# Four modulation units in one run of products behind one weight unit, where they stood as two pairs

## Chip, core and metric

One Trainium2 chip, one of its cores. The metric is the device time of one execution, in microseconds (us). The kernel works on float32 data throughout.

## What is computed

Two transformer blocks, one after the other, on 256 positions of width 2048. The first has a mixer (a gated linear recurrence and sparse attention), a feed-forward part and a gated extra input. The second has two layers that work on two streams, x and a context, and each scales, shifts and gates both by numbers that it makes from two vectors, `c` and `c_ctx`: the modulation. Cut to what the change touches:

```python
# first block, feed-forward part
f = jnp.square(jax.nn.relu(rms_norm(h, norm_mlp_pre[i]) @ mlp_w1[i])) @ mlp_w2[i]
h = h + rms_norm(f, norm_mlp_post[i])
...
# second block, for each of its two layers l
shift, scale, gate = jnp.split((s_lat @ w_mod[l] + b_mod[l])[:, None, :], 3, axis=-1)
shift_c, scale_c, gate_c = jnp.split(s_ctx @ w_mod[l] + b_mod[l], 3, axis=-1)
hx = _rmsnorm(x, norm_g[l]) * (1.0 + scale) + shift
hc = _rmsnorm(ctx, norm_g[l]) * (1.0 + scale_c) + shift_c
```

`w_mod` is 2048 x 6144 for each layer. Nothing of it depends on the feed-forward part, so the kernel makes most of it beside that part.

## The kernel before

All weights stream from HBM through a ring of four slots, `raw`, in **units** of 1 MB (128 partitions x 4 tiles of rows x 512 columns). `HAND` is the list of all units in the order in which SyncE (SP) fetches them; SP issues unit n only when unit n - 4, which had the same slot, is done with.

There are two kinds of unit. A **weight unit** is split in two halves of its own: ScalarE (ACT) makes the rounded high part `whi` (line 1415, two instructions, one for each half), VectorE (DVE) makes the rest, `wlo` (line 2001), and the slot is free when the second low half is made (`lo_ready`). `whi` and `wlo` have two places each, so a half is split only when TensorE (PE) has used the same half of the weight unit two before (`unit_used`). PE then runs 24 products of 128x512 (`hand_unit`, lines 724 to 726). A **modulation unit** is not split: PE multiplies the raw float32 tiles by two columns of `cvec` (`mod_products`, line 772, four products that lie side by side in the array), and the slot is free when they are done (`plain_used`). The profile has two records for each of these products, so a unit is 8 records there and a pair is 16.

The feed-forward part has 128 weight units, n = 0 to 127 (even groups of 16 from the up projection `mlp_w1`, odd ones from the down projection `mlp_w2`). From n = 4 on they are counted in groups of seven, m_ = (n - 4) // 7 and at = (n - 4) % 7. Each group m_ = 0 to 15 makes one chunk of 512 columns of `w_mod` out of four modulation units. For m_ = 0 to 11 PE does it, into PSUM bank 3; the last four (`SUMS`) are summed on DVE. Behind the fourth unit:

- for m_ = 0 to 3 (`ROWS`) ACT copies two rows out and DVE adds them (`mod_row`);
- for m_ = 4 to 11 (`COLS`) ACT copies the bank to `modp_b` (line 1433) and PE turns it by four transposes (line 779). The transposes stand behind the weight unit with at = 5. The copy stands in ACT's program behind the split of the weight unit with at = 6.

```python
                if at == 6 and m_ in COLS:
                    mod_part(MODSS + m_, MOD1[4 * m_ + 3], modp_b, 3)
```

ACT's loop over the weight units n does first `hand_split(x)`, then `beside(n - 2)` (small work for the attention of the context: exponentials at line 1697, squares at line 1710), then the line above. PE too has such small work behind some weight units (lines 1029 to 1132).

Of the kernel before, what the change touches and what calls it, by code (L numbers as in the profile page):

```python
# [41 lines left out]
MODSS = 2 * D // CH  # L42
# [6 lines left out]
MODB = [(0, MODSS + i) for i in range(MODCH - MODSS)] + [(1, i) for i in range(MODCH)]  # L49
# [13 lines left out]
STEP_AT = [13 + 3 * n // 2 for n in range(len(STEP))] + [37, 38, 39]  # L63
N_VEC, N_CONST = 1 + 18 + 2, 3 + 4
MOD1_AT = 4
SUM_AT = (1, 2, 4, 5)
MOD0_AT = [(3 + 4 * m, 4 + 4 * m, 5 + 4 * m, 5 + 4 * m) for m in range(8)]

# [29 lines left out]
def build(nc, I, out):  # L98
    ctx = ExitStack()
    with ctx:  # L100
# [347 lines left out]
        order = []  # L448
# [2 lines left out]
        order += ["in2_0c"] * 5 + ["cmp", "in2_0c", "in2_0c"] * 4 + ["in2_0c"] * 35  # L451
        order += ["out1"] * 16 + ["in2_0c"] * 4
        for n in range(128):
            order += ["mlp"] + (["mod1"] * 2 if MOD1_AT <= n < 7 * len(MODB) + MOD1_AT and (n - MOD1_AT) % 7 in (1, 4) else [])
        order += ["out2_0c"] * 8 + ["gate", "gate", "pp", "gate", "gate"] * 4 + ["out2_0c"] * 8
        for l in range(2):
            order += (["in2_1c"] * 16 if l else []) + [f"in2_{l}x"] * 52 + [f"out2_{l}"] * 16
# [16 lines left out]
        SUMS = [m_ for m_, (l, col) in enumerate(MODB) if l and col >= MODSS]  # L474

        def before(those, m_):
            return len([i for i in those if i < m_])
# [100 lines left out]
        def ev(name):  # L578

            if name not in one_shot:  # L580
                one_shot[name] = sem(name)
            return one_shot[name]
# [106 lines left out]
        def _(pe):  # L689
# [17 lines left out]
            def hand_unit(x, A, middle=None):  # L707

                hi_, lo_ = A
                by_rows = x.u in (0, UPC - 1) and x.s > 0  # L710
                for i in range(2 * TB):
                    b, kh = (i // 2, i % 2) if by_rows else (i % 2, i // 2)
                    a, bank = half(x, b)
                    if b == 0:
                        pe.wait_ge(lo_ready, 2 * x.s + kh + 1)
                    if x.u == 0 and a >= 3 and kh == 0:
                        pe.wait_ge(half_out, a - 2)
                    if i == 2 and middle is not None:
                        middle()
                    tt = slice(b * P, b * P + P)  # L720
                    dst = ps[:, bank, :]
                    for k in range(2 * kh, 2 * kh + 2):
                        kk, nth = UK * x.k + k, UK * x.u + k
                        mm(dst, hi_[:, kk, tt], whi[:, x.s % 2, k, :], start=(nth == 0), stop=False)  # L724
                        mm(dst, hi_[:, kk, tt], wlo[:, x.s % 2, k, :], start=False, stop=False)  # L725
                        ins = mm(dst, lo_[:, kk, tt], whi[:, x.s % 2, k, :], start=False, stop=(nth == KT - 1))  # L726
                    if x.u == UPC - 1 and (b, kh) == (0, 1):
                        ins.then_inc(half_done, 1)
                    if b == 1:
                        ins.then_inc(unit_used, 1)  # L730
# [37 lines left out]
            def mod_products(y, bank):  # L768

                pe.wait_ge(raw_in[y.slot], y.landed)  # L770
                for k in range(UK):
                    ins = mm(ps[32 * k:32 * k + 32, bank, :], cvec[:, UK * y.u + k, :], raw[:, y.slot, k],  # L772
                             start=(y.u == 0), stop=(y.u == UPC - 1))
                ins.then_inc(plain_used, 1)

            def mod_columns(modp, bank):

                for j in range(4):
                    ins = nc.tensor.transpose(ps[:, bank, j * P:j * P + P], modp[:, j * P:j * P + P], eye[:, :])
                ins.then_inc(ev("modc_sum"), 1)  # L780
# [240 lines left out]
            def turn(x, c):  # L1021

                zp = (x.i // 8 * 4 + c) % 2
                pe.wait_ge(relu_sq, 2 * (x.i // 8 * 4 + c + 1))
                if x.i or c:
                    pe.wait_ge(hT_lo, x.i // 8 * 4 + c)
                for k in range(UK):
                    for b in range(TB):
                        ins = nc.tensor.transpose(ps[:, 4 + k // 2, ((k % 2) * TB + b) * P:((k % 2) * TB + b + 1) * P],  # L1029
                                                  zst[:, zp, b, k * P:k * P + P], eye[:, :])  # L1030
                ins.then_inc(hT_psum, 1)
# [113 lines left out]
            for n, x in enumerate(MLP):  # L1145
                q, j = x.i // 8, x.i % 8
                if x.u == 2 and 1 <= j <= 4:
                    turn(x, j - 1)
                if x.i == 0:
                    pe.wait_ge(a_lo, PR["mlp"]["t0"] + 2 * (x.u + 1))  # L1150
                if j == 4:
                    pe.wait_ge(hT_lo, q * 4 + x.u + 1)
                hand_unit(x, AX_ if j < 4 else AY_)
                m_, at = (n - MOD1_AT) // 7, (n - MOD1_AT) % 7
                if at == 5 and m_ in SUMS:
                    pe.wait_ge(plain_used, MOD1[4 * m_ + 3].p + 1)
                    pe.wait_ge(ev("modc_set"), MODSS + len(COLS))
                    pe.wait_ge(ev("mod_row"), len(ROWS) - len(SUMS))
                    pe.wait_ge(ev("mod_part"), before(ROWS, m_))
                    mm(ps[0:32, 3, :], ones[:, 0:32], modp_b, start=True, stop=True).then_inc(ev("modc_sum"), 1)  # L1160
                if 0 <= m_ < SUMS[0] and at in (1, 4):
                    if at == 1 and m_:
                        pe.wait_ge(ev("modc_set"), MODSS + before(COLS, m_))
                        pe.wait_ge(ev("mod_row"), before(ROWS, m_))
                    for u in ((0, 1) if at == 1 else (2, 3)):
                        mod_products(MOD1[4 * m_ + u], 3)
                elif m_ in COLS and at == 5:
                    pe.wait_ge(ev("modp_in"), MODSS + before(COLS, m_) + 1)
                    mod_columns(modp_b, 3)
                beside(n)  # L1170
                if n == 120:
                    pe.wait_ge(ev("p_in"), 16)
                    for k in range(2):
                        for b in range(TB):
                            ins = nc.tensor.transpose(ps[:, 3, (k * TB + b) * P:(k * TB + b + 1) * P],
                                                      prow[:, b, k * P:k * P + P], eye[:, :])
                    ins.then_inc(ev("pT_made"), 1)
# [192 lines left out]
        def _(act):  # L1370
# [270 lines left out]
            def hT_part(c):  # L1641

                act.wait_ge(hT_psum, c + 1)
                act.wait_ge(unit_used, 2 * MLP[32 * (c // 4)].s)
                A(ay_hi[:, UK * (c % 4):UK * (c % 4) + UK, :].rearrange("p (a b) c -> p a (b c)", b=2), ps[:, 4:6, :],
                  ACT.Copy).then_inc(hT_hi, 1)
# [104 lines left out]
            for n, x in enumerate(MLP):  # L1751
# [3 lines left out]
                if n % 4 == 3 and 1 <= x.i % 8 <= 4:  # L1755
                    hT_part(x.i // 8 * 4 + x.i % 8 - 1)
                m_, at = (n - MOD1_AT) // 7, (n - MOD1_AT) % 7
                if at == 6 and m_ in COLS:
# [195 lines left out]
        def _(dve):  # L1954
# [541 lines left out]
            def mod_sum(m_, y):  # L2496

                dve.wait_ge(raw_in[y.slot], y.landed)
                dve.wait_ge(plain_used, y.p)
                if y.u == 0:  # L2500
                    dve.wait_ge(ev("modc_sum"), MODSS + len(COLS) + before(SUMS, m_))
                for k in range(UK):
                    w, c_ = raw[:, y.slot, k], cvec[:, UK * y.u + k, 0:1]
                    if y.u == 0 and k == 0:
                        ins = V.tensor_scalar(modp_b, w, c_, None, ALU.mult)
                    else:
                        ins = V.scalar_tensor_tensor(out=modp_b, in0=w, scalar=c_, in1=modp_b, op0=ALU.mult, op1=ALU.add)  # L2507
                    if k < UK - 1:
                        link(ins)
                ins.then_inc(plain_used, 1)  # L2510

            early, beside = Beside(c_maxima()), Beside(context())
            for n, x in enumerate(MLP):
# [5 lines left out]
                beside(n - 2)  # L2519
                m_, at = (n - MOD1_AT) // 7, (n - MOD1_AT) % 7  # L2520
                if at == 1 and m_ - 1 in COLS:
                    mod_set(1, MODB[m_ - 1][1], MODSS + before(COLS, m_))
                if m_ in SUMS and at in SUM_AT:
                    mod_sum(m_, MOD1[4 * m_ + SUM_AT.index(at)])
                if at == 6 and m_ in ROWS and m_ not in SUMS:
# [240 lines left out]
        def _(pool):  # L2766
# [145 lines left out]
            for i in range(8 * FF_Q):  # L2912
# [4 lines left out]
                for m_ in ROWS:  # L2917
                    if i == (7 * m_ + MOD1_AT + 8) // 4 + 1:
                        l, col = MODB[m_]
# [143 lines left out]
```

## Time and profile before

| | us |
|---|---|
| median of three runs | 2708.12 |
| lowest and highest of them | 2706.82, 2709.78 |
| the profiled execution | 2708.84 |
| span in its profile | 2707.0 |
| PE busy in the span | 2680.8 |
| granted TensorE clock, mean | 0.998 of full speed |

The profiled execution is 0.72 us above the median and 1.84 us above its own span. A group of rows for a line of the kernel gives how often it ran, what one took, and how long its engine was idle just ahead of it. In a timeline the first number is the start and the second how long the row lasted; matmuls are pipelined, so the start of the next one tells what one costs, not its length.

### The profile page before, as it was taken

How to read it: one execution, taken by the hardware profiler on the slowest of the kernel's cores; microseconds unless marked ns; L12 is line 12 of the kernel's file. 1: busy time of each engine (PE TensorE's matmuls, PEld its weight loads, DVE VectorE, ACT ScalarE, POOL GpSimd, SP SyncE). 2: the span in 40 equal slices, each digit the busy share in tenths (PEclk: the TensorE clock that was granted, in tenths of full speed). 3: DMA queues.
4: the chain of work that ended last, by engine and by line, in shares of the span. 5: the costliest groups of instructions: out<-in, count | busy, mean ns of one | idle time of the engine just before them, and what ended most of it. 6: DMA issues, size and time to landing. Idle time of an engine off the chain costs nothing.

```text
span 2707.0 us, 32331 instructions
## 1 busy us (share of the span) xinstructions
PE 2680.8 (99%) x12942; PEld 2130.5 (79%) x12942; DVE 1815.5 (67%) x2438; ACT 1303.3 (48%) x1893; POOL 337.8 (12%) x308
## 2 busy tenths in 40 slices
PE   9999999999999999999999999999999999999998
PEld 7676777788877777777778888888778888877787
DVE  5647766765666666665877665668886764788865
ACT  5353445554544344344534444455555454555554
POOL 0000100000131010010010300223300111432001
PEclk9999999999999999999999999999999999999999
DMA  9878575465678776777877765655445656554453
GB/s 321 299 276 310 171 251 183 167 231 199 235 267 301 253 250 228 258 248 264 305 243 270 266 218 202 220 198 186 140 155 180 211 186 198 171 177 139 171 185 139
DMA packets 293158, 600.30 MB, mean 222 GB/s; under 512 B 12530, under 2 KB 19386, under 8 KB 291088
## 3 DMA queue, kind: packets, MB, share of 16 engines
q1 hardware_dynamic: 279856, 547.81, 58.9%
q0 software_dynamic: 10624, 46.93, 4.7%
q10 hardware_dynamic: 2528, 3.49, 0.4%
q8 instruction: 103, 1.69, 0.3%
q14 instruction: 47, 0.39, 0.0%
HBM read 585.02 MB, written 13.17 MB: 221 GB/s over the span
## 4 chain that ended last, share of the span: by engine, by line
PE 93%; DVE 3%; DMA 2%; SPq 0%; issue 0%; ACT 0%; DVEq 0%; ACTq 0%
PE ps L724 27%; PE ps L726 26%; PE ps L725 26%; PE ps L772 3%; DVE wlo L2001 1%; PE ps L1240 1%; DMA raw<-in_w_in_dram 1%; PE ps L1200 1%; PE ps L704 1%; DMA raw<-in_mlp_w_dram 1%; PE ps L962 1%; PE ps L1068 1%; PE ps L1029 1%; PE ps L1208 1%; PE ps L1298 1%; PE ps L994 1%
## 5 line engine op out<-in xcount | busy, mean ns | idle before, releaser
L2001 DVE TENSOR_TENSOR wlo<-raw,whi 128x1024 fp32r<-128x1024 f32 x834 | 1051.7, 1288 | 662.6 <-ACT whi L1415 658.4
L1415 ACT ACTIVATE whi<-raw 128x1024 fp32r<-128x1024 f32 x834 | 865.4, 1056 | 1052.8 <-PE ps L726 708.1
L724 PE MATMUL ps<-whi,ay_hi 128*128 128x512 f32 x1712 | 681.1, 398 | 1.3 <-DVE zsc L2317 1.2
L726 PE MATMUL ps<-whi,ay_lo 128*128 128x512 f32 x1712 | 667.7, 390 | 0.0
L725 PE MATMUL ps<-wlo,ay_hi 128*128 128x512 f32 x1712 | 667.0, 390 | 0.0
L724 PE MATMUL ps<-whi,ax_hi 128*128 128x512 f32 x1600 | 639.7, 400 | 9.3 <-DVE wlo L2001 7.4
L726 PE MATMUL ps<-whi,ax_lo 128*128 128x512 f32 x1600 | 624.8, 390 | 0.0
L725 PE MATMUL ps<-wlo,ax_hi 128*128 128x512 f32 x1600 | 624.1, 390 | 0.0
L724 PEld LDWEIGHTS ps<-whi,ay_hi 128*128 128x128 f32 x1712 | 321.6, 188 | 84.6 <-issue 17.6
L724 PEld LDWEIGHTS ps<-whi,ax_hi 128*128 128x128 f32 x1600 | 300.9, 188 | 101.0 <-issue 25.0
L726 PEld LDWEIGHTS ps<-whi,ay_lo 128*128 128x128 f32 x1712 | 321.3, 188 | 68.5
L725 PEld LDWEIGHTS ps<-wlo,ay_hi 128*128 128x128 f32 x1712 | 321.9, 188 | 63.2
L726 PEld LDWEIGHTS ps<-whi,ax_lo 128*128 128x128 f32 x1600 | 300.7, 188 | 64.8
L725 PEld LDWEIGHTS ps<-wlo,ax_hi 128*128 128x128 f32 x1600 | 301.3, 188 | 58.4
L2629 DVE SCALAR_TENSOR_TENSOR bvx<-ucx,cols,bvx 128x256 f32<-128x256 f32 x240 | 136.3, 629 | 0.0
L2931 POOL TENSOR_TENSOR zst<-zst 128x512 f32<-128x512 f32 x32 | 46.1, 1446 | 413.6 <-DVE zst L2378 413.5
L1823 ACT ACTIVATE ex<-ps,stx 128x512 f32<-128x512 f32 x64 | 43.4, 684 | 89.3 <-PE ps L1208 70.6
L772 PE MATMUL ps<-raw,cvec 128*32 128x512 f32 x640 | 78.6, 600 | 0.0
L2572 DVE TENSOR_REDUCE stx<-ps 128x2 f32<-128x1024 f32 x32 | 39.1, 1222 | 31.4 <-PE ps L1240 31.4
L2810 POOL DMA_DIRECT2D z2c<-zsc x13 | 9.4, 726 | 392.7 <-DVE zsc L2317 392.7
L2417 DVE SCALAR_TENSOR_TENSOR cbv<-cuc,cols,cbv 128x256 f32<-128x256 f32 x120 | 50.0, 478 | 0.0
L2507 DVE SCALAR_TENSOR_TENSOR modp_b<-raw,cvec,modp_b 128x512 f32<-128x512 f32 x60 | 45.1, 751 | 3.1 <-DMA raw<-in_w_mod_dram 1.4
(533 smaller groups left out, 1995.8 us busy)
## 6 DMA issues: line engine op xcount, KB each, us to landing
raw<-in_w_in_dram SPq DMA_DIRECT2D x207, 1024.0 KB, 5.1
raw<-in_mlp_w_dram SPq DMA_DIRECT2D x128, 1024.0 KB, 7.0
raw<-in_w_mod_dram SPq DMA_DIRECT2D x96, 1024.0 KB, 8.9
raw<-in_w_out_dram SPq DMA_DIRECT2D x64, 1024.0 KB, 5.1
raw<-in_ple_gate_dram SPq DMA_DIRECT2D x16, 1024.0 KB, 5.1
z2c<-zsc POOLq DMA_DIRECT2D x13, 512.0 KB, 3.1
G<-bias_d ACTq DMA_DIRECT2D x4, 768.0 KB, 7.0
h<-in_ctx_dram POOLq DMA_DIRECT2D x1, 2048.0 KB, 10.3
```

The costliest lines, as they stand in the source:

```text
L724: mm(dst, hi_[:, kk, tt], whi[:, x.s % 2, k, :], start=(nth == 0), stop=False)
L725: mm(dst, hi_[:, kk, tt], wlo[:, x.s % 2, k, :], start=False, stop=False)
L726: ins = mm(dst, lo_[:, kk, tt], whi[:, x.s % 2, k, :], start=False, stop=(nth == KT - 1))
L772: ins = mm(ps[32 * k:32 * k + 32, bank, :], cvec[:, UK * y.u + k, :], raw[:, y.slot, k], start=(y.u == 0), stop=(y.u == UPC - 1))
L1415: A(part(whi[:, x.s % 2], x, kh), part(raw[:, x.slot], x, kh), ACT.Copy).then_inc(hi_ready, 1)
L1823: ins = A(W.e[:, j % 2, c_, :], ps[:, 3 + c_, :], ACT.Exp, scale=0.125, bias=stx[:, j % 4, c_:c_ + 1], accum_out=stx[:, j % 4, 2 + c_:3 + c_])
L2001: V.tensor_tensor(part(wlo[:, x.s % 2], x, kh), part(raw[:, x.slot], x, kh), f32v(part(whi[:, x.s % 2], x, kh)), ALU.subtract).then_inc(lo ...
L2417: ins = V.scalar_tensor_tensor(out=cbv[:, g, :], in0=cuc[:, g, tap:tap + SEQ], scalar=w, in1=cbv[:, g, :], op0=ALU.mult, op1=ALU.add)
L2507: ins = V.scalar_tensor_tensor(out=modp_b, in0=w, scalar=c_, in1=modp_b, op0=ALU.mult, op1=ALU.add)
L2572: link(V.tensor_reduce(stx[:, j % 4, 0:2], ps[:, 3:5, :], AX.X, ALU.max))
L2629: ins = V.scalar_tensor_tensor(out=bvx[:, g, :], in0=ucx[:, g, tap:tap + SEQ], scalar=w, in1=bvx[:, g, :], op0=ALU.mult, op1=ALU.add)
L2931: TT(t_, t_, t_, ALU.mult).then_inc(relu_sq, 1)
```

## The change

For the groups 0 to 11 (`WHOLE` is 12) the four modulation units stand together. In SP's order they come behind the weight unit with at = 5; on PE their 32 records (16 products in the program) come behind the weight unit with at = 4. The four groups that are summed on DVE keep their two pairs.

```diff
@@ -63,6 +63,7 @@
 MOD1_AT = 4
+WHOLE = next(m for m, (l, col) in enumerate(MODB) if l and col >= MODSS)
 SUM_AT = (1, 2, 4, 5)
@@ -451,7 +452,11 @@
         for n in range(128):
-            order += ["mlp"] + (["mod1"] * 2 if MOD1_AT <= n < 7 * len(MODB) + MOD1_AT and (n - MOD1_AT) % 7 in (1, 4) else [])
+            m_, at = (n - MOD1_AT) // 7, (n - MOD1_AT) % 7
+            if 0 <= m_ < WHOLE:
+                order += ["mlp"] + ["mod1"] * (4 if at == 5 else 0)
+            else:
+                order += ["mlp"] + ["mod1"] * (2 if WHOLE <= m_ < len(MODB) and at in (1, 4) else 0)
@@ -1158,11 +1163,11 @@
-                if 0 <= m_ < SUMS[0] and at in (1, 4):
-                    if at == 1 and m_:
+                if 0 <= m_ < WHOLE and at == 4:
+                    if m_:
                         pe.wait_ge(ev("modc_set"), MODSS + before(COLS, m_))
                         pe.wait_ge(ev("mod_row"), before(ROWS, m_))
-                    for u in ((0, 1) if at == 1 else (2, 3)):
+                    for u in range(4):
                         mod_products(MOD1[4 * m_ + u], 3)
```

SP's queue over one group of the feed-forward part, before: each row is a fetch into `raw`, with what SP waits for ahead of it.

```order
L668 DMA raw<-in_w_mod_dram 128x4x512 [waits lo_ready] x2
L676 DMA raw<-in_mlp_w_dram 128x4x512 [waits lo_ready] x2
L676 DMA raw<-in_mlp_w_dram 128x4x512 [waits plain_used]
L668 DMA raw<-in_w_mod_dram 128x4x512 [waits plain_used]
L668 DMA raw<-in_w_mod_dram 128x4x512 [waits lo_ready]
L676 DMA raw<-in_mlp_w_dram 128x4x512 [waits lo_ready] x2
L676 DMA raw<-in_mlp_w_dram 128x4x512 [waits plain_used] x2
```

The same stretch of SP's queue after the change (the lines of the file have moved down by five).

```order
L681 DMA raw<-in_mlp_w_dram 128x4x512 [waits lo_ready] x3
L673 DMA raw<-in_w_mod_dram 128x4x512 [waits lo_ready] x4
L681 DMA raw<-in_mlp_w_dram 128x4x512 [waits plain_used] x4
L681 DMA raw<-in_mlp_w_dram 128x4x512 [waits lo_ready] x3
L673 DMA raw<-in_w_mod_dram 128x4x512 [waits lo_ready] x4
```

The four `w_mod` units stand in a row, and the four weight units behind them (at = 6, 0, 1 and 2) each wait until PE has used the modulation unit that had their slot.

PE's program at the first pair of group 6 (behind the weight unit with at = 1), before.

```order
L724 MATMUL ps<-whi,ax_hi 128x512
L725 MATMUL ps<-wlo,ax_hi 128x512
L726 MATMUL ps<-whi,ax_lo 128x512
L772 MATMUL ps<-raw,cvec 32x512 x8
L1088 MATMUL ps<-cv,caT 128x128 x2
L724 MATMUL ps<-whi,ay_hi 128x512
```

The same place after: the pair is gone, and the small work stands right behind the weight unit.

```order
L729 MATMUL ps<-whi,ax_hi 128x512
L730 MATMUL ps<-wlo,ax_hi 128x512
L731 MATMUL ps<-whi,ax_lo 128x512
L1093 MATMUL ps<-cv,caT 128x128 x2
L729 MATMUL ps<-whi,ay_hi 128x512
```

And behind the weight unit with at = 4, after, where the second pair was.

```order
L731 MATMUL ps<-whi,ay_lo 128x512
L777 MATMUL ps<-raw,cvec 32x512 x16
L1093 MATMUL ps<-cv,caT 128x128 x2
L729 MATMUL ps<-whi,ay_hi 128x512
L730 MATMUL ps<-wlo,ay_hi 128x512
```

All 16 products of the group stand there. ACT's program is the same before and after; this is its piece for group 6, where `raw_in1` tells of the landing of the weight unit with at = 6.

```order
L1415 ACTIVATE whi<-raw 128x1024 [waits unit_used,raw_in1]
L1415 ACTIVATE whi<-raw 128x1024 [waits unit_used]
L1697 ACTIVATE ce,cst<-ps,cst 128x256 [waits d_aT,d_max]
L1697 ACTIVATE ce,cst<-ps,cst 128x256
L1433 ACTIVATE modp_b<-ps 128x512 [waits modc_sum,plain_used]
```

The copy to `modp_b`, for which PE's four transposes wait, comes behind both halves of that split and behind the exponentials.

## Rows read from the trace of the kernel before

**Rows 1.** The page, part 1: busy time of the engines.

```profile
PE 2680.8 (99%) x12942; PEld 2130.5 (79%) x12942; DVE 1815.5 (67%) x2438; ACT 1303.3 (48%) x1893; POOL 337.8 (12%) x308
```

**Rows 2.** Busy time by window, groups 4 to 11: length, engines, clock, DMA, GB/s.

```profile
925.00:1290.00 365.00, 365.00 (x1827) 282.59 (x1826) 226.57 (x345) 153.63 (x240) 26.74 (x22) 1.00 0.71 249
```

**Rows 3.** Timeline of PE around a run of one modulation unit: start, length.

```profile
186.05 0.39 PE L726 MATMUL ps<-whi,ax_lo 128*128 128x512 f32 x1
...
187.36 0.50 PE L724 MATMUL ps<-whi,ax_hi 128*128 128x512 f32 x1
```

**Rows 4.** Timeline of PE around a pair with a weight unit behind it.

```profile
798.98 0.39 PE L726 MATMUL ps<-whi,ax_lo 128*128 128x512 f32 x1
...
801.15 0.50 PE L724 MATMUL ps<-whi,ax_hi 128*128 128x512 f32 x1
...
802.43 0.39 PE L726 MATMUL ps<-whi,ax_lo 128*128 128x512 f32 x1
```

**Rows 5.** Timeline of PE, second pair of group 6, on to its transposes.

```profile
1049.49 0.39 PE L726 MATMUL ps<-whi,ay_lo 128*128 128x512 f32 x1
...
1050.17 0.39 PE L726 MATMUL ps<-whi,ay_lo 128*128 128x512 f32 x1
1050.49 1.92 PE L772 MATMUL ps<-raw,cvec 128*32 128x512 f32 x16
1052.34 0.71 PE L1088 MATMUL ps<-cv,caT 128*128 128x128 f32 x4
1052.81 0.47 PE L724 MATMUL ps<-whi,ay_hi 128*128 128x512 f32 x1
...
1058.38 0.60 PE L779 MATMUL ps<-eye,modp_b 128*128 128x128 f32 x4
```

**Rows 6.** Timeline around the end of a weight unit with no run behind it.

```profile
969.24 0.40 PE L726 MATMUL ps<-whi,ax_lo 128*128 128x512 f32 x1
...
969.48 0.61 PE L1088 MATMUL ps<-cv,caT 128*128 128x128 f32 x4
...
969.84 0.48 PE L724 MATMUL ps<-whi,ax_hi 128*128 128x512 f32 x1
...
972.02 0.37 SPq L676 DMA_DIRECT2D raw<-in_mlp_w_dram  x1
```

**Rows 7.** Timeline of PE: small work behind the second pair of group 5.

```profile
1003.61 0.70 PE L1068 MATMUL ps<-cqk 128*128 128x256 f32 x2
...
1004.71 0.48 PE L724 MATMUL ps<-whi,ax_hi 128*128 128x512 f32 x1
```

**Rows 8.** Timeline of SP: first fetch that the second pair of group 6 frees.

```profile
1051.61 0.37 SPq L676 DMA_DIRECT2D raw<-in_mlp_w_dram  x1
```

**Rows 9.** DMA issues at 1051.6, at 955.3 and at 1124.1: KB, us to landing.

```profile
raw<-in_mlp_w_dram SPq DMA_DIRECT2D x1, 1024.0 KB, 5.2
...
raw<-in_mlp_w_dram SPq DMA_DIRECT2D x1, 1024.0 KB, 5.6
...
raw<-in_mlp_w_dram SPq DMA_DIRECT2D x1, 1024.0 KB, 7.0
```

**Rows 10.** Timeline of ACT: a whole split; exponentials and the copy; a square.

```profile
1044.03 2.01 ACT L1415 ACTIVATE whi<-raw 128x1024 fp32r<-128x1024 f32 x2 [4.94 <-DMA raw<-in_mlp_w_dram]
...
1051.56 0.46 ACT L1697 ACTIVATE ce<-ps,cst 128x256 f32<-128x256 f32 x1
...
1052.48 0.60 ACT L1433 ACTIVATE modp_b<-ps 128x512 f32<-128x512 f32 x1
...
1060.77 0.30 ACT L1710 ACTIVATE flip<-cq 128x128 f32<-128x128 f32 x1
```

**Rows 11.** Timeline of DVE: an evacuation, low halves behind one, low halves beside GpSimd.

```profile
1058.58 0.69 DVE L2384 TENSOR_TENSOR yb<-ps,yb 128x512 f32<-128x512 f32 x1 [2.04 <-PE ps L726]
1059.19 2.35 DVE L2001 TENSOR_TENSOR wlo<-raw,whi 128x1024 fp32r<-128x1024 f32 x2
...
794.63 3.20 DVE L2001 TENSOR_TENSOR wlo<-raw,whi 128x1024 fp32r<-128x1024 f32 x2
```

## Prediction

> **What bounds the kernel now.** I read the page first: PE is busy for 99% of the span [rows 1]. That is an average, so I then took the busy time by windows over the part that the change touches. In the 365 us of groups 4 to 11 PE is busy for all 365 us at the full clock, while the DMA engines are busy for 0.71 of the time at 249 GB/s [rows 2]. PE waits for nothing there, so whatever shortens its program shortens the kernel, until something makes it wait. Third, the timeline of PE around the runs, for what a run costs beyond its products. Last, the timelines of SP, ACT and DVE and the fetches, for how late each may be. The reader is to see two things: a small fixed price for each run, and a chain from PE's use of a slot to the next weights in `whi` that is about as long as the time which the new order leaves for it.
>
> **What the change removes.** The start of a row on PE tells the cost. Weight products follow each other by (1050.17 - 1049.49) / 3 = 0.227 us [rows 5]. From the last weight product ahead of a run to the first behind it: 187.36 - 186.05 = 1.31 us for one modulation unit [rows 3], 801.15 - 798.98 = 2.17 us for two [rows 4]. So a further unit costs 0.86, and four take 2.17 + 2 x 0.86 = 3.89. Before, a group paid 2 x 2.17 = 4.34; after, it pays 3.89 and one ordinary step of 0.227 at the place that has become empty. Saved: 0.22 us.
>
> What stands behind the run starts slowly too. Five weight products behind a pair take 802.43 - 801.15 = 1.28 us, where five steps are 1.14: 0.14 more [rows 4]. Four small products at line 1088 take 1052.81 - 1052.34 = 0.47 behind a pair [rows 5] and 969.84 - 969.48 = 0.36 behind a weight unit [rows 6]: 0.11 more. At the place of the first pair, weight products follow in six of the twelve groups (1, 2, 3, 4, 8, 11) and small work in the other six. The saving is 6 x (0.22 + 0.14) + 6 x (0.22 + 0.11) = **4.1 us**. It is all on PE, which is the path.
>
> No product, copy, transpose or byte is added or taken away: 48 modulation units before and after, and PE's waits for `modc_set` and `mod_row` only move from at = 1 to at = 4, later than what they wait for.
>
> **What it moves.** SP's order decides when slots come free. Let R be the start of a run, so that PE leaves the run at R + (1052.34 - 1050.49) + 2 x 0.86 = R + 3.57 [rows 5].
>
> *The weight unit with at = 6.* It now has the slot of the group's first modulation unit, and SP fetches it when PE has used that one: 1051.61 - 1050.49 = 1.12 us after R [rows 5, 8]. Behind it, its landing takes 5.2 us from an idle queue for a down projection, 5.6 for an up projection [rows 9]; ACT splits both halves in 2.01 [rows 10]. In the kernel before, the same fetch went out before the second pair, and its split was done before PE came there. Queued behind ACT's wait for the landing is, in groups 4 to 11, the copy to `modp_b`, 0.60 us, with the small work ahead of it: exponentials, 1052.48 - 1051.56 = 0.92, in groups 6, 7 and 10; a square of 0.30 in groups 4 and 8 [rows 10]. I take 0.08 for the two hand-overs by semaphore (an estimate: 1058.38 to 1058.58 is 0.2 with a product's end in it, so 0.08 may be low) [rows 5, 11]. PE waits for that copy behind the very next weight unit. PE is there at R + (1058.38 - 1050.49 - 0.47) + 2 x 0.86 = R + 9.14 [rows 5], plus the small work behind the run: none in groups 4, 7, 8; 0.47 in 6 and 10; 1004.71 - 1003.61 = 1.10 in 5 and 9 [rows 7].
> - Groups 6 and 10 (down): copy done at 1.12 + 5.2 + 2.01 + 0.92 + 0.60 + 0.08 = 9.93, PE at 9.61: wait 0.32 each.
> - Group 7 (down): 9.93 against 9.14: 0.79.
> - Groups 4 and 8 (up): 1.12 + 5.6 + 2.01 + 0.30 + 0.60 + 0.08 = 9.71 against 9.14: 0.57 each.
> - Groups 5 and 9 (up, with one small piece on ACT, taken at an exponential's 0.46): 9.87 against 10.24: none. Group 11 (down, none): 9.01 against 9.14: none.
> Sum 2.6 us. The unit itself is needed only after the transposes, and its first low half is ready at about R + 1.12 + 5.6 + 1.0 + 1.2 = R + 8.9 (half of [rows 10] and of the 2.35 in [rows 11]), so in groups 0 to 3 the wait is 0 by this.
>
> *The fourth modulation unit.* It has the slot of the weight unit with at = 5, which is split only when PE is done with at = 3. From that moment to SP's next fetch are 972.02 - 969.48 = 2.54 us [rows 6], then 5.2 to land (the nearest idle-queue row; no `w_mod` fetch with an idle queue is shown) [rows 9]: 7.74. PE wants it after 24 x 0.227, the 0.09 by which a run starts late (1050.49 - 1050.17 - 0.227) and three units of 0.86: 8.12 [rows 5]. The margin is 0.38. In groups 0, 4 and 8 DVE has an evacuation of 0.69 to do first, and where GpSimd squares beside it (0 and 4) two low halves take 3.20 and not 2.35 [rows 11]: late by 1.2 in groups 0 and 4, by 0.3 in group 8. What is late here no longer is late at the transposes, since the fetch for at = 6 is out before. It adds 1.2 (group 0), 1.2 - 0.57 = 0.6 (group 4), 0 (group 8): 1.8.
>
> Waits: 2.6 + 1.8 = **4.4 us**. Sum: -4.1 + 4.4 = +0.3, on the profiled execution's 2708.84, which is 0.72 over the median: 2709.1 as a profile, **2708.4** as a median. A change of 0.2% (5.4 us) is about what a measurement of this kernel can tell from none.
>
> **Bounds.** Below: no waits at all, -4.1. Above: every such fetch takes the 7.0 us of the third row of [rows 9], 1.8 and 1.4 more for down and up. Then groups 6, 7, 10 and 11 wait 2.1, 2.6, 2.1 and 1.7, groups 4, 8, 5 and 9 wait 2.0, 2.0, 1.0 and 1.0, and groups 0 to 3 about 1.4 each for the late modulation unit (1.8 less the margin of 0.38): some 20 us, +16. Near which end? Two of three rows are at 5.2 and 5.6, and these fetches go out singly, 0.86 us apart, with the fourth modulation unit's landing just over. I take 5.2 and 5.6. In a stretch with full DMA engines a fetch lands 3.0 us after the one ahead (1.05 MB at 249 / 0.71 = 351 GB/s) [rows 2]; the fourth modulation unit lands at about R + 2.2, so R + 5.2 is no later than R + 6.3 and does not bind.
>
> At this place the Trainium skill can be set beside the trace. "DMA: Bandwidth & Descriptors", section "Anatomy of one DMA — SWDGE (gpsimd) path", gives a fixed 2.0 us plus the bytes over 436 GB/s, 4.4 us for such a fetch. The trace shows 5.2 and more for fetches of SP's queue [rows 9], so it does not agree; by the page's figure nearly every wait above would be gone, and the time would be that of rival one.
>
> **Rivals.**
> 1. *The waits are hidden, the saving stays.* The landing is 0.8 us shorter than I take (4.4), or PE's small work covers it: For it: margins are a few tenths. Against it: the shortest landing of [rows 9] is 5.2. Time 2708.12 - 4.1 = 2704.0. Chance 0.20.
> 2. *Slower.* Mechanism: ACT's copy to `modp_b` behind the split of the weight unit with at = 6, whose fetch now starts at R + 1.12. If that fetch shares the DMA engines with the fourth modulation unit, it takes up to 7.0, as the third row of [rows 9] does. It decides from 5.4 + 4.1 = 9.5 us of waits, 0.8 a group, which is reached when landings are about 0.7 us longer than I take. Time by the upper bound 2708.12 + 16 = 2724, halfway 2716. Chance 0.22.
> 3. *The run does not cost less.* The fixed price belongs to each unit, not to each run, and 3.89 is 4.34. Against it: 1.31 and 2.17 are not in the ratio of one to two [rows 3, 4]. Time 2708.12 + 4.4 = 2712.5. Chance 0.06.
>
> **How the numbers follow.** The forecast (the saving and waits of 2 to 7 us, 2706 to 2711) has 0.52. The median is taken at 2708.4. The range reaches down to rival one's 2704.0 less half a microsecond of measurement, 2703.5, and up to rival two's halfway point, 2716; outside are about 0.07 below and 0.12 above. Faster by over 0.2% (under 2702.7) would need more than the whole saving: 0.07. Slower by over 0.2% (over 2713.5): rival two, 0.22, and a little of rival three: 0.23. Within: 0.70.
>
> **What the changed profile would show.** The run: from the weight product ahead to the first behind 3.9 us, 32 records. PE idle ahead of its transposes in groups 4, 6, 7, 8 and 10, by 0.3 to 0.8 us, released by ACT's copy; none in 5, 9 and 11. PE idle inside the run in groups 0 and 4, released by a landing of `w_mod`. ACT waits for landings of `mlp_w` at at = 6. SP's fetch for at = 6 at R + 1.12, landing in 5.2 to 5.6. The prediction is wrong if that landing takes over 6 us, if a copy on ACT has another wait ahead of it, or if small work on PE at other places waits for ACT, whose whole program is now behind the landing.

## The result and the profile after

The changed kernel takes 2720.31 us (median of 5 runs, 2717.06 to 2723.0) where the kernel before takes 2708.12: 1.0045 times as long, with a 95% interval of 1.0034 to 1.0055. That is 12.2 us slower, 4.3 us beyond the upper end of the forecast's range. A second measurement, on another chip, gave 2716.6 and 1.003 [1.0018, 1.0042], so 8 to 12 us is the size to explain.

The page of the changed kernel, its span and its first part, whose columns are busy us, share of the span and instructions:

```profile
span 2718.0 us, 32331 instructions
PE 2681.1 (99%) x12942; PEld 2132.9 (78%) x12942; DVE 1815.4 (67%) x2438; ACT 1303.4 (48%) x1893; POOL 341.0 (13%) x308
```

Instructions and busy time are those of [rows 1]; the span is 11.0 us longer. Of that, 1.08 lies ahead of the feed-forward part, where the two kernels have the same order: its first weight product starts at 721.90 and not at 720.83, and in the other profiles below at 719.4 to 723.5. That difference belongs to the execution. The other 9.95 us arise inside the part, which ends at 1554.63 and not at 1543.60. The waits of PE from 720 to 1300 (in total, times, longest, us) say where to look:

```profile
PE ps L729 <- DVE wlo L2006: 3.4, 1, 3.4
PE ps L784 <- ACT modp_b L1438: 2.5, 2, 1.9
PE ps L777 <- DMA raw<-in_w_mod_dram: 1.4, 2, 1.0
PE ps L1084 <- DVE ce L2436: 1.0, 1, 1.0
```

In the kernel before PE had none in this stretch. The second and third row are the two kinds of wait that the forecast priced. The first and the fourth it had at zero. (In these rows `modp_b` is the copy for PE's transposes, `wlo` a low half, `ce` the scaled exponentials.) The timeline of PE in group 1 (start, us, engine, line, operation) shows the largest:

```profile
819.84 0.39 PE L731 MATMUL ps<-whi,ax_lo 128*128 128x512 f32 x1
820.16 3.64 PE L777 MATMUL ps<-raw,cvec 128*32 128x512 f32 x32
823.73 0.50 PE L729 MATMUL ps<-whi,ay_hi 128*128 128x512 f32 x1
...
829.08 0.39 PE L731 MATMUL ps<-whi,ay_lo 128*128 128x512 f32 x1
832.90 0.77 PE L729 MATMUL ps<-whi,ay_hi 128*128 128x512 f32 x1 [3.43 <-DVE wlo L2006]
833.46 0.63 PE L730 MATMUL ps<-wlo,ay_hi 128*128 128x512 f32 x1
...
838.58 0.41 PE L730 MATMUL ps<-wlo,ay_hi 128*128 128x512 f32 x1
```

The run takes 823.73 - 819.84 = 3.89 us, as forecast. One weight unit later PE stands for 3.43 us, until DVE has the low half of the unit with at = 6. And then the products come at 833.89 - 833.46 = 0.43 us each, where they come at 0.23 elsewhere. That is the clock. Here are windows over that place and over group 7 (PE, PEld, DVE, ACT and POOL busy, then the granted clock, the DMA engines' share and GB/s):

```profile
829.00:832.90 3.90, 0.47 (x4) 0.08 (x2) 1.38 (x2) 2.46 (x3) 0.00 (x0) 0.85 1.04 387
832.90:836.00 3.10, 3.10 (x7) 2.45 (x8) 3.07 (x6) 2.02 (x3) 0.00 (x0) 0.50 1.04 386
836.00:841.00 5.00, 5.00 (x18) 3.98 (x17) 4.93 (x6) 1.06 (x1) 0.51 (x1) 0.74 0.73 268
841.00:850.00 9.00, 9.00 (x46) 7.52 (x45) 6.42 (x9) 4.09 (x4) 0.00 (x0) 1.00 0.65 233
...
1112.00:1115.50 3.50, 1.56 (x9) 1.06 (x8) 2.95 (x4) 3.50 (x8) 0.00 (x0) 0.94 1.04 386
1115.50:1119.00 3.50, 3.50 (x11) 2.82 (x11) 3.46 (x7) 1.25 (x2) 0.00 (x0) 0.57 1.04 387
```

TensorE had stood idle; after it the granted clock was 0.50, the lower of its two levels (1.2 of 2.4 GHz), and it came back to full within 836 to 841: from 838.58 on the products come 0.25 us apart and less, 5.7 us after PE had resumed. The unit with at = 6 took 9.02 us where the same unit took 6.24 before: the clock costs 2.78 us there, on top of the wait. After 1.94 us of idleness in group 7 the clock is 0.57 for a while, and the unit behind it takes 1.42 more.

Why was that weight unit late? The DMA issues at 817 to 821.5 (KB, us to landing), of the changed kernel:

```profile
cq<-z2c POOLq DMA_DIRECT2D x1, 1024.0 KB, 7.0
raw<-in_mlp_w_dram SPq DMA_DIRECT2D x1, 1024.0 KB, 9.1
ck<-z2c POOLq DMA_DIRECT2D x1, 512.0 KB, 7.6
cv<-z2c POOLq DMA_DIRECT2D x1, 512.0 KB, 9.4
```

The fetch goes out at 821.29, R + 1.13 as forecast, but GpSimd has issued 2 MB of loads for the context work 2.7 to 4.2 us earlier (at 817.13, 817.89 and 818.62). The fetch takes 9.1 us and not 5.2. The same view of the kernel before, at 815 to 822, already has this:

```profile
cq<-z2c POOLq DMA_DIRECT2D x1, 1024.0 KB, 5.5
raw<-in_mlp_w_dram SPq DMA_DIRECT2D x1, 1024.0 KB, 8.3
ck<-z2c POOLq DMA_DIRECT2D x1, 512.0 KB, 6.1
cv<-z2c POOLq DMA_DIRECT2D x1, 512.0 KB, 8.6
```

There the fetch of 8.3 us is the one that the second pair of group 1 frees, for the weight unit with at = 0 of the next group. Two weight units stood between them, and PE did not feel it. None of the landings on which the forecast rests is from this stretch [rows 9].

Group 7, on PE and then on ACT, has the copy chain that the forecast did describe:

```profile
1112.58 0.39 PE L731 MATMUL ps<-whi,ay_lo 128*128 128x512 f32 x1
1114.91 1.00 PE L784 MATMUL ps<-eye,modp_b 128*128 128x128 f32 x4 [1.94 <-ACT modp_b L1438]
1115.56 0.77 PE L729 MATMUL ps<-whi,ay_hi 128*128 128x512 f32 x1
```

```profile
1111.45 2.01 ACT L1420 ACTIVATE whi<-raw 128x1024 fp32r<-128x1024 f32 x2 [12.97 <-DMA raw<-in_mlp_w_dram]
1113.37 0.45 ACT L1702 ACTIVATE ce<-ps,cst 128x256 f32<-128x256 f32 x1
...
1113.82 0.46 ACT L1702 ACTIVATE ce<-ps,cst 128x256 f32<-128x256 f32 x1
...
1114.27 0.59 ACT L1438 ACTIVATE modp_b<-ps 128x512 f32<-128x512 f32 x1
```

The landing, the split of 2.01, the exponentials of 0.90 and the copy of 0.59 stand in one line, and PE waits for the end. The landing took 6.6 us here, where 5.2 was assumed:

```profile
raw<-in_mlp_w_dram SPq DMA_DIRECT2D x1, 1024.0 KB, 6.6
```

Unit by unit, against the kernel before, the feed-forward part reads: group 1 +6.3 (3.55 in the unit with the wait, 2.78 in the slow one); group 7 +3.8 (2.34 and 1.42); inside the runs of groups 0 and 4 +1.9 (waits of 0.98 and 0.46, and each run goes on 0.21 later than its wait explains: 5.08 - 3.89 - 0.98 in group 0); group 3 +1.2; groups 2, 6, 8, 10, 11 and a unit of group 12 +2.6; the run itself -3.8; and -2.0 in group 13, which the change does not touch. That makes 10.0, where 9.95 were measured.

Of the 2.0 in group 13, 1.6 are the clock once more. Both kernels wait 1.8 us there, at the same product; these are PE's rows in the kernel before and in the changed one, and the windows behind them (in each pair the kernel before stands first):

```profile
1375.91 0.68 PE L724 MATMUL ps<-whi,ax_hi 128*128 128x512 f32 x1 [1.80 <-DVE zst L2378]
1388.50 0.50 PE L729 MATMUL ps<-whi,ax_hi 128*128 128x512 f32 x1 [1.81 <-DVE zst L2383]
```

```profile
1376.07:1379.48 3.41, 3.41 (x9) 2.63 (x10) 3.41 (x3) 0.67 (x1) 3.38 (x3) 0.50 0.88 234
1388.00:1393.00 5.00, 4.50 (x17) 2.85 (x18) 5.00 (x5) 2.12 (x2) 3.53 (x3) 1.00 0.78 226
```

In the kernel before, the clock was at its lower level for 3.4 us behind that wait, and the weight unit took 13.69 us; in the changed kernel's first profile it stayed at full speed, and the unit took 12.11. In the second profile it took 13.70. So this difference belongs to the execution and not to the change.

### The profile page after: what moved, and what is told of

It reads as the page before. It is cut to its first block, busy times and chain, and to the rows that moved or that the text cites. A ratio compares the mean times of both kernels' runs of the same rounds, so it can differ in the third digit from the quotient of the medians.

```text
span 2718.0 us, 32331 instructions
## 1 busy us (share of the span) xinstructions
PE 2681.1 (99%) x12942; PEld 2132.9 (78%) x12942; DVE 1815.4 (67%) x2438; ACT 1303.4 (48%) x1893; POOL 341.0 (13%) x308
## 4 chain that ended last, share of the span: by engine, by line
PE 90%; DVE 5%; DMA 4%; ACT 1%; issue 1%; SPq 1%; DVEq 0%; ACTq 0%
PE ps L729 26%; PE ps L731 25%; PE ps L730 25%; DMA raw<-in_mlp_w_dram 2%; DVE wlo L2006 2%; PE ps L777 2%; PE ps L1245 1%; PE ps L1205 1%; DMA raw<-in_w_in_dram 1%; PE ps L709 1%; PE ps L967 1%; PE ps L1034 1%; PE ps L1213 1%; ACT whi L1420 1%; PE ps L1303 1%
## 5 line engine op out<-in xcount | busy, mean ns | idle before, releaser
L777 PEld LDWEIGHTS ps<-raw,cvec 128*32 128x32 f32 x640 | 16.9, 109 | 41.6 <-issue 36.4
```

## Experiments

Each was timed against the kernel before on its own chip. Times of different experiments differ by chip and by execution, as the two measurements of the changed kernel do (3.7 us), so each is read first by its ratio and then by where PE waits in its profile. One length in the profiles is steadier than the times: that of groups 0 to 11, from the first weight product of group 0 to that of group 12. It is 1298.17 - 742.59 = 555.58 us in the kernel before, the same 555.58 in experiment 10, whose order of work is that of the kernel before, and 567.10 in the changed kernel, 11.5 more. It is given below as "groups 0 to 11".

**1. The copy ahead of the split.** One block of ACT's program moves, so that `modp_b` no longer stands behind the late landing.

```diff
 for n, x in enumerate(MLP):
+    m_, at = (n - MOD1_AT) // 7, (n - MOD1_AT) % 7
+    if at == 6 and m_ in COLS:
+        mod_part(MODSS + m_, MOD1[4 * m_ + 3], modp_b, 3)
     if n >= 2:
         hand_split(x)
...
-    m_, at = (n - MOD1_AT) // 7, (n - MOD1_AT) % 7
-    if at == 6 and m_ in COLS:
-        mod_part(MODSS + m_, MOD1[4 * m_ + 3], modp_b, 3)
```

> The changed kernel, with ACT's copy to modp_b (groups 4 to 11) ahead of the split of the weight unit with at = 6 and no longer behind it. If the copy behind the late landing is what PE waits for, the idle time ahead of the transposes (1.94 us in group 7, 0.53 in group 8 of the changed kernel) goes, and with it the slow clock behind group 7's (1.4 us): 2720.3 - 3.5, about 2717. The rival, that the landing of the same weight unit binds just behind it, leaves a wait ahead of that unit's first product in its place: landing at R + 7.8, low half at R + 10.2, PE there at R + 9.6, so 0.6 us in group 7, and the time stays within 1.5 us of 2720.

Measured: 2716.73 us, 1.0032 [1.0021, 1.0044]. Waits of PE from 720 to 1300:

```profile
PE ps L729 <- DVE wlo L2006: 4.5, 2, 4.2
PE ps L1084 <- DVE ce L2436: 2.2, 3, 1.0
PE ps L777 <- DMA raw<-in_w_mod_dram: 1.3, 2, 0.9
```

The row of `modp_b` is gone, so the copy chain is what made PE wait at the transposes. The wait of group 1 stays, 4.2 us here behind a landing of 9.9. Part of the wait comes back one step on: in group 7, with a landing of 6.57, the transposes start unhindered at 1112.06 and the weight products then wait 0.34 for the low half, and in groups 6 and 8 the exponentials' scaling is 0.6 late. The time does not settle what this is worth, since 1.0032 lies between the two measurements of the changed kernel. Groups 0 to 11 take 565.14 us, 9.6 over the kernel before. Most of the loss stays: it is not in the copy.

**2. Group 1 alone in two pairs.** The order of slots and the products follow the kernel before in this group only.

```diff
+RUN = [m for m in range(WHOLE) if m != 1]
...
-            if 0 <= m_ < WHOLE:
+            if m_ in RUN:
                 order += ["mlp"] + ["mod1"] * (4 if at == 5 else 0)
...
-                    for u in range(4):
+                    for u in range(4) if m_ in RUN else ((0, 1) if at == 1 else (2, 3)):
```

> The changed kernel, with group 1 alone as two pairs again. In the profile of the changed kernel group 1 has 3.43 us of idle PE ahead of the weight unit with at = 6, and 2.78 us of slower products behind it; both should go, and 0.4 us of saving with them: 2720.3 - 5.8, about 2714.5. The rival, that the wait moves to the next group (the DMA engines are behind by the same bytes), leaves the time at 2720.

Measured: 2715.55 us, 1.0026 [1.0015, 1.0037]. Waits of PE from 720 to 1300:

```profile
PE ps L785 <- ACT modp_b L1439: 3.5, 3, 1.9
PE ps L778 <- DMA raw<-in_w_mod_dram: 1.4, 2, 1.0
PE ps L1085 <- DVE ce L2437: 1.0, 1, 1.0
```

The wait of 3.4 and the slow clock behind it are gone, and no wait of that size came up in another group; the copy's waits stay, with 3.5 us in three groups. Groups 0 to 11 take 560.28 us, 4.7 over the kernel before. The time alone would not show this, since it is only 1.0 us under the second measurement of the changed kernel (2716.6).

**3. GpSimd's loads later.** The run stays in all twelve groups. The three loads go out three context steps later, after the fetch of group 1 has landed.

```diff
                     pool.wait_ge(ev("e_pool"), 4)
+                if i == 5:
                     dma(cq[:, :, :], z2v[:, :, 0:1024]).then_inc(ev("e_in"), 16)
```

> The changed kernel, with GpSimd's three loads of context rows (cq, ck, cv, 2 MB together) issued some 20 us later, behind the row sums of group 1, and so not in the run of group 1. If these loads make the fetch in group 1 take 9.1 us where the other groups have 5.0 to 6.6, it lands in 5.2 here, and the time falls by 3.4 + 2.8 us, to about 2714. If something else delays it (the unit's place in HBM, the fetches queued behind it), the time stays at 2720 and the idle time in group 1 with it.

Measured: 2713.76 us, 1.0022 [1.0014, 1.0031]. The landing in group 1 takes 5.8 us. The timeline of PE there:

```profile
826.70 0.39 PE L731 MATMUL ps<-whi,ay_lo 128*128 128x512 f32 x1
827.21 0.47 PE L729 MATMUL ps<-whi,ay_hi 128*128 128x512 f32 x1
```

Between them lie 0.51 us where 0.23 is a step: the wait of 3.43 has become 0.12. Groups 0 to 11 take 560.37 us, 4.8 over the kernel before; the time is 6.6 us under the first measurement of the changed kernel and 2.8 under the second. Since nothing of the run was changed, this shows that the stall of group 1 came from the loads that share the DMA engines with the fetch.

**4. Filler products in the wait.** In the place where it stood idle in group 1, PE runs 14 products of no use (28 records of the profile). They are not meant to shorten the wait; they only keep TensorE at work.

```diff
+                if m_ == 1 and at == 5:
+                    pe.wait_ge(ev("c_poolo"), 1)
+                    warm(14)
```

> The changed kernel, with 14 extra products of 128x128 ones on PE (about 3.1 us, result unused) in group 1, behind the weight unit with at = 5, where PE is idle for 3.43 us. The wait stays. If the idle time is what brings the granted clock down to half behind it, the 2.78 us of slower products go and the time falls to about 2717.5. If the clock falls for another reason, the time stays at 2720 or grows.

Measured: 2714.09 us, 1.0023 [1.0014, 1.0033]. Timeline and window of PE:

```profile
827.80 3.29 PE L793 MATMUL ps<-ones 128*128 128x128 f32 x28
830.84 0.48 PE L729 MATMUL ps<-whi,ay_hi 128*128 128x512 f32 x1
831.15 0.40 PE L730 MATMUL ps<-wlo,ay_hi 128*128 128x512 f32 x1
```

```profile
831.00:837.00 6.00, 6.00 (x31) 4.96 (x31) 5.90 (x10) 3.37 (x4) 0.51 (x1) 1.00 1.04 384
```

The weight products behind the filler run at 0.23 us each, at a granted clock of 1.00. The DMA engines are as full as in the changed kernel (1.04 in both), so the 0.43 us a product there were the clock and not contention. The weight unit with at = 6 of group 1 costs 0.14 us more than in the kernel before, where it cost 2.78. Groups 0 to 11 take 561.05 us, 5.5 over the kernel before. Not all of the gain is the clock: in this execution the fetch of group 1 took 8.4 us and not 9.1, and those of groups 6 and 7 took 5.2 and 5.1.

**5 and 6. The changed kernel and the filler again, side by side.** The same two kernels on one chip, because the changed kernel had not been in the same comparison as experiment 4.

> The changed kernel once more, on the same chip as g2_warm_again, for a second profile of it. Group 1's wait of some 3.4 us and the slow clock behind it should be there again, since the same loads collide. Whether group 7's landing (6.64 us in the first profile, 5.1 to 6.7 in the others) is again late tells if that wait belongs to the order or to the single execution. Median 2719 to 2721.

> The kernel of e4_warm once more, beside the changed kernel. By the slow products of group 1 alone the difference is 2.8 us; e4_warm stood 6 us under the changed kernel's first median, in another run of the comparison. If the difference is 2.5 to 3.5 us here, the rest was spread between the runs; if it is 6 again, the filler removes more than the slow clock.

Measured: 2716.6 us, 1.003 [1.0018, 1.0042], for the changed kernel; 2713.5 us, 1.002 [1.0011, 1.0029], with the filler. The changed kernel was expected at 2719 to 2721 and came out below that. The intervals overlap, but the medians are 3.1 us apart, within the 2.5 to 3.5 that were expected, and the unit that runs slowly in the changed kernel's profile costs 2.6 there (2.78 in the first profile, 0.12 with the filler), with a wait of 3.5 us after a landing of 9.22. Groups 0 to 11 take 565.89 us, 10.3 over the kernel before, and 560.87 with the filler. This difference of 5.0 is more than the clock, since the filler's execution also had the earlier landings (8.60 in group 1, 5.07 and 5.05 in groups 6 and 7, where the changed kernel had 6.20 and 6.40). In group 7 this execution shows something else (the transposes, then the window behind them):

```profile
1115.03 0.66 PE L784 MATMUL ps<-eye,modp_b 128*128 128x128 f32 x4 [1.70 <-ACT modp_b L1438]
```

```profile
1115.00:1119.00 4.00, 3.97 (x20) 3.36 (x21) 3.96 (x9) 1.87 (x2) 0.00 (x0) 1.00 1.04 386
```

PE was idle for 1.70 us and the clock stayed at 1.00. In experiment 2 it stayed so after 1.93 us, where the first profile had 0.57 after 1.94. So an idleness of this length at this place costs the clock in one execution and not in another, as the 1.8 us in group 13 do.

**7. Both cures together**, the copy first and the loads later.

> The changed kernel with both cures at once: the copy to modp_b ahead of the split of the weight unit with at = 6, and the three context loads behind the row sums of group 1. If the two waits are separate and add up, the time is 2720.3 - 3.6 - 6.5 = 2710. If they are one delay that is handed on, it stays near the better of the two, 2713.8.

Measured: 2712.58 us, 1.0014 [1.0005, 1.0024], 2.6 over what was expected. What stays are the late fourth modulation unit in groups 0 and 4 (1.6 us), the exponentials in group 3 and one other (1.6), and the low halves (1.2: 0.72 in group 1, 0.44 in group 7). Groups 0 to 11 take 558.90 us, 3.3 over the kernel before.

**8. As 7, with groups 0, 3 and 4 in pairs.** `RUN = (1, 2, 5, 6, 7, 8, 9, 10, 11)` in the place where experiment 2 has its list.

> As f1_both, but groups 0, 3 and 4 keep their two pairs: those in which, in the profiles with both cures' parts, PE still waits (inside the run in 0 and 4, by 1.0 and 0.4 us; 1.2 us behind the row sums in 3). The other nine groups are one run each. The saving of nine runs is 2.7 us and about 1.5 us of waits are left: 2707.6 - 1.2, about 2706.5, no change that can be measured. If the changed order costs something that no wait shows, it stays at 2709 or more.

Measured: 2709.06 us, 1.0005 [0.9996, 1.0014]; its span is 2705.9, with 1.1 us of waits in this stretch. It ties with the kernel before. Nine runs should save some 2.6 us (0.3 to 0.4 in seven groups, under 0.05 in groups 5 and 9) and the waits shown take 1.1 back. Yet groups 0 to 11 take 556.01 us, 0.4 more than in the kernel before: the shorter span comes from group 13, which the change does not touch and where a wait of 1.80 us is 0.22 in this execution. The time of 2709.06 is on the side of "2709 or more" that was to tell of a cost that no wait shows. Where the rest of the saving goes is not settled. No version was found that beats the kernel before.

**9 and 10. The fetch cut to a quarter.** In the changed kernel and in the kernel before, the fetch of the weight unit with at = 6 brings only the first of its four parts in groups 0 to 11; the rest of the slot keeps old data, so neither computes the reference's feed-forward part. The products and splits are all there.

```diff
+                    m = (UPC * x.i + x.u - MOD1_AT)
+                    if 0 <= m < 7 * 12 and m % 7 == 6:
+                        sp.dma_start(raw[:, x.slot, 0:1], src[:, 0:1]).then_inc(raw_in[x.slot], 16)
+                    else:
                         sp.dma_start(raw[:, x.slot], src).then_inc(raw_in[x.slot], 16)
```

> The changed kernel, with the fetch of the weight unit with at = 6 in groups 0 to 11 cut to its first quarter (256 KB instead of 1 MB; the rest of the slot keeps old data, so the feed-forward result is not the reference's). To be read against f4_cut_pairs, the kernel before with the same cut. If the lost saving is the lateness of this one fetch, it lands some 2 us earlier, the waits at the transposes and in group 1 go, and this is faster than f4_cut_pairs by the saving less the late modulation units and the row sums: 3.9 - 2.6 = about 1.3 us, so no slower. If the loss has another cause (bytes in flight in general, DVE or ACT order), this stays some 10 us slower than f4_cut_pairs.

> The kernel before, with the same 12 fetches cut to a quarter as in f3_cut_run (the feed-forward result is not the reference's). PE waits for no landing in the feed-forward part of the kernel before, so the time stays at 2707.6, within 1.5 us, by both theories.

Measured: 2709.37 us, 1.0005 [0.9996, 1.0014], with the run; 2707.62 us, 1.0001 [0.9992, 1.001], with pairs. Of the 8 to 12 us 1.8 are left, so most of the loss goes when this one fetch is cut. The cut also takes 9 MB off the DMA engines, and these two runs do not tell a shorter fetch from emptier engines. The run was expected to come out 1.3 us ahead and did not: groups 0 to 11 take 558.72 us against 555.58. Its waits from 720 to 1300:

```profile
PE ps L781 <- DMA raw<-in_w_mod_dram: 3.4, 2, 2.4
PE ps L733 <- DVE wlo L2010: 1.1, 1, 1.1
```

All waits for the copy are gone. In group 4 the fourth modulation unit took 7.07 us to land, where it took 5.10 in the changed kernel; PE waited 2.43 inside the run, and in the window from 960 to 963 the granted clock was 0.76. Why that unit came late when less was fetched is open. The last row is group 1, where a quarter of this fetch still takes 6.75 us beside GpSimd's loads.

**11. Single units.** The kernel before with groups 0 to 11 in four runs of one unit each, behind at = 1, 2, 3 and 4 (one of the lines that change):

```diff
-                    for u in ((0, 1) if at == 1 else (2, 3)):
+                    for u in (at - 1,):
```

> The kernel before, with each group's two pairs (groups 0 to 11) split into four runs of one modulation unit, behind the weight units with at = 1, 2, 3 and 4. 24 runs more, and 1.31 + 1.31 - 2.17 = 0.45 us each less an ordinary step of 0.227, plus 0.11 to 0.14 for what stands behind: 24 x 0.33 = 8 us if the fixed price belongs to the run, so about 2715.5. If it belongs to the unit (the rival of the prediction), the time stays at 2707.6. More than 2718 would tell of a new wait.

Measured: 2715.57 us, 1.0031 [1.0018, 1.0043], and no wait of PE. One of the runs, in PE's timeline:

```profile
767.07 0.39 PE L726 MATMUL ps<-whi,ax_lo 128*128 128x512 f32 x1
767.39 1.06 PE L772 MATMUL ps<-raw,cvec 128*32 128x512 f32 x8
768.38 0.50 PE L724 MATMUL ps<-whi,ax_hi 128*128 128x512 f32 x1
```

From the weight product ahead to the first behind it takes 1.31 us, as in [rows 3]. Twenty-four more runs cost 7.6 us, 0.32 each (0.20 to 0.48 by the interval), with the same products; groups 0 to 11 take 563.91 us, 8.3 more. The fixed price belongs to the run and not to its length.

## Why the prediction was wrong

The direction of the sum was named as rival two, at 0.22; the forecast of "within" failed. Point by point:

- **The saving was right.** A run takes 3.89 us, as worked out. Ten groups save 0.3 to 0.4 each, but groups 5 and 9 under 0.05, where 0.33 was put: 3.8 in all against 4.1. Experiment 11 shows the mechanism, and rival three falls.
- **The copy to `modp_b` was right in kind, and in size but for one group.** The copy ended at R + 9.56 to R + 9.78 in groups 4, 5, 6, 8, 9 and 10, where 9.71 to 9.93 was worked out. PE waited 0.53 in group 8 (0.57), 0.2 in 6 and 0.1 in 10 (0.32), none in 5, 9 and 11 (none). In group 7 it was 1.94 where 0.79 was forecast, because the landing took 6.6 us. Experiment 1 shows that this chain is the cause.
- **The late fourth modulation unit was right in kind.** PE waited 0.98 for it in group 0 (1.2) and 0.46 in group 4 (also 1.2, of which the sum added 0.6), and not at all in group 8 (0.3). It landed at R + 3.72 and R + 3.20. As forecast, group 4 then had no wait at its transposes.
- **The failed step is the landing**: "Near which end? Two of three rows are at 5.2 and 5.6, and these fetches go out singly [...] I take 5.2 and 5.6", and from it "so in groups 0 to 3 the wait is 0 by this". In ten of twelve groups the fetch took 5.0 to 5.8 us. In group 1 it took 9.1, because GpSimd's loads were under way, and that is above even the upper bound of 7.0. The forecast counted only SP's fetches as sharing the DMA engines, though the trace of the kernel before had 8.3 us for a fetch at this place. Experiments 2 and 3 show the cause from two sides. The chain itself was right: with 9.13 in the place of the landing, the low half is ready at R + 1.12 + 9.13 + 1.0 + 1.2 = R + 12.45, and PE is there at R + 9.14, a wait of 3.3 where 3.43 was measured. The upper bound left this term out as well: with its 7.0 the low half comes at R + 10.3, already 1.2 late in groups 1 and 3. The forecast had named the sign, "wrong if that landing takes over 6 us". In the other direction, no whole fetch of 1 MB at this place landed in less than 5.0 us in any of these runs, so the 4.4 of rival one was never seen.
- **A term was missing: the clock.** The sum counted a wait as its length. The wait of 3.43 us in group 1 cost 2.78 more, and the one in group 7 1.42 more: 4.2 us on top of the 8.3 us of waits in this stretch. Experiment 4 shows it for group 1. The trace of the kernel before had an example, the 1.6 us behind the wait of 1.80 in group 13.
- **Group 3.** Here the landing was as assumed (5.1 us), and ACT then loads a table, makes exponentials and copies the modulation row; DVE's adds and low halves follow, and PE waits 1.02 for the scaled exponentials. "Small work on PE at other places waits for ACT" was named as what would make the prediction wrong, but not priced. It is 1.2 us. That the same order of work makes it late is read from the timelines; no experiment changed it alone.
- **Rival two** came true in its sign and in its point of decision: 9.5 us of waits were asked for, and the waits of this stretch and the clock make 12.5 (8.3 and 4.2). Its mechanism did so only in part. It has the copy late in every group, sharing DMA with the fourth modulation unit; what decided was one group, another engine's loads, the low half and not the copy, and the clock.

What stays open is why the landing in groups 6 and 7 varies: 5.2 and 6.6 us in the first profile, 6.20 and 6.40 in the second, and 5.05 and 5.14 in group 7 in the two kernels with filler. Nor was it settled when an idleness of 1.7 to 2.6 us costs the clock. The two measurements of the changed kernel, 2720.3 and 2716.6, are not explained by their profiles either: the executions profiled took 2719.84 and 2719.74, the second of which was the slowest of its six runs. The account by groups above is thus that of an execution 3 us above the second median.

## What to carry to other kernels

When an order change turns a transfer that nobody waited for into one with a margin of a few tenths, take the landing time of each of its places from the trace, with everything that all queues issue in the microseconds before, and not one typical landing for all. Where PE has been busy without a gap, price a new wait of several microseconds at more than its length, because the granted clock can fall behind it: here 3.4 us cost 6.2. And a saving of 0.35 us a group is soon eaten when the same edit puts an in-order engine's small copy behind a landing.

## What the runs showed of the hardware

- After 3.43 us without products TensorE's granted clock was at its lower level (0.50) and full again 5.7 us after it had resumed; products took 0.43 us where they take 0.23. With 14 filler products (28 records) in the gap it stayed at 1.00.
- After waits of 1.7 to 2.6 us the granted clock fell in some executions and not in others: to 0.50 for 3.4 us behind 1.80 in the kernel before, and not behind 1.81 at the same product in the changed kernel; 0.57 over 3.5 us behind 1.94 in group 7, and 1.00 behind 1.70 and 1.93 there; 1.00 also behind a wait of 2.60 at 1359.73 in experiment 4. Where it fell, it cost 1.4 to 1.6 us more than the wait.
- The fetch of 1 MB behind a run took 5.0 to 5.8 us in most groups and at most 6.7 where GpSimd loaded nothing beside it. In group 1 beside 2 MB of GpSimd's loads it took 8.4 to 9.9, and a quarter of it there still 6.75. In group 7 it was seen at 5.05 and at 6.64 in different executions.
- A run of 32-column float32 products among the weight products has a fixed price of about 0.32 us; runs of one, two and four units (8, 16 and 32 records) take 1.31, 2.17 and 3.89 us. A single run of 32 products saves only 0.3 to 0.4 us against two of 16 where weight products or the small work at line 1088 follow, and under 0.05 in groups 5 and 9.
